# Output projection in three split passes through the piece ring, and a filter layer of two full-depth passes

## The reference

```python
merged = sigmoid(g_diff) * (o_diff @ w_proj_diff) + sigmoid(g_mla) * (o_mla @ w_proj_mla)
x = x + merged @ w_out                      # 512x1024 @ 1024x1024: the output projection
...
h = sin(freq * (h @ f_w3 + f_b3))           # 512x64
h = (h @ f_wout).reshape(L, 2, D_MODEL)     # the filter's last layer, 64 deep
h = h * exp(-t * |deltas|)                  # the decay
```

## Time and profile before

| | us |
|---|---|
| median of 3 runs (lowest, highest) | 1130.77 (1129.69, 1133.97) |
| the profiled execution | 1134.14 |
| its span | 1132.2 |
| merging of the attentions ends on PE | about 412.9 |
| first tile of the output projection | 414.70 to 421.64 |
| first turned tile of the next stage | 508.11 |

### The profile page before, as it was taken

How to read it: one execution, slowest core, us unless ns; L and a number is a source line. 1 busy time by engine, 2 the same in 40 slices (tenths; PEclk the granted TensorE clock), 3 DMA queues, 4 the chain that set the end, 5 groups by cost and what they waited for, 6 DMA issues and landing times.

```text
span 1132.2 us, 13210 instructions
## 1 busy us (share of the span) xinstructions
PE 1084.9 (96%) x4906; PEld 852.2 (75%) x4906; DVE 663.4 (59%) x1006; ACT 398.7 (35%) x624; POOL 513.9 (45%) x383
## 2 busy tenths in 40 slices
PE   6999989999899999998999989989999999999996
PEld 5889877766777864446788877867888888888885
DVE  6554759875487652388487784447666666640203
ACT  5223645453554201353443333143322223231211
POOL 1067989999200001150543335443555455464441
PEclk9999999999999999899999999989999999999999
DMA  6246354242344940330221211321222212322421
GB/s 243 75 159 227 109 211 160 84 159 85 130 149 164 372 157 0 130 130 1 93 75 75 76 75 72 151 94 67 84 75 106 116 74 83 139 75 75 149 75 75
DMA packets 17782, 131.41 MB, mean 116 GB/s; under 512 B 2289, under 2 KB 2689, under 8 KB 11138
## 3 DMA queue, kind: packets, MB, share of 16 engines
q1 hardware_dynamic: 8720, 93.21, 21.9%
q0 software_dynamic: 6560, 27.27, 7.2%
q10 hardware_dynamic: 2450, 10.21, 2.3%
HBM read 124.40 MB, written 6.29 MB: 115 GB/s over the span
## 4 chain that ended last, share of the span: by engine, by line
PE 87%; DVE 6%; ACT 3%; DMA 2%; issue 1%; POOL 1%; SPq 0%; ACTq 0%; POOLq 0%; DVEq 0%
PE bank L484 70%; PE bank L475 9%; PE bank L490 2%; PE bank L705 2%; DMA ring<-weights_in 1%; PE bank L703 1%; PE bank L702 1%; PE bank L851 1%; DMA x_sb<-x_in 1%; PE bank L820 1%; ACT arena L1070 1%; POOL ring_parts L1533 0%; ACT arena L1045 0%; PE bank L707 0%; ACT arena L1181 0%
## 5 line engine op out<-in xcount | busy, mean ns | idle before, releaser
L1533 POOL TENSOR_TENSOR ring_parts<-ring,ring_parts 128x1024 fp32r<-128x1024 f32 x98 | 237.8, 2430 | 299.2 <-ACT ring_parts L1045 298.9
L484 PE MATMUL bank<-hT_parts,ring_parts 128*128 128x512 f32 x1344 | 340.4, 394 | 0.5 <-ACT hT_parts L1317 0.5
L1045 ACT ACTIVATE ring_parts<-ring 128x1024 fp32r<-128x1024 f32 (+2 forms) x155 | 160.4, 1041 | 478.0 <-PE bank L484 298.5
L484 PEld LDWEIGHTS bank<-hT_parts,ring_parts 128*128 128x128 f32 x1344 | 250.5, 189 | 54.4 <-issue 2.4
L484 PE MATMUL bank<-ring_parts,arena_parts 128*128 128x512 f32 (+1 forms) x672 | 155.7, 386 | 1.5 <-DVE arena L2124 0.8
L484 PE MATMUL bank<-arena_parts,ring_parts 128*128 128x512 f32 x592 | 147.8, 391 | 2.9 <-DVE arena L1715 2.6
L484 PEld LDWEIGHTS bank<-ring_parts,arena_parts 128*128 128x128 f32 x672 | 124.5, 188 | 27.2 <-DVE arena L2124 1.3
L484 PE MATMUL bank<-ring_parts,hT_parts 128*128 128x512 f32 (+1 forms) x544 | 138.7, 379 | 0.3
L2227 DVE SCALAR_TENSOR_TENSOR arena<-bank,small,arena 128x441 f32<-128x441 f32 (+2 forms) x176 | 122.3, 695 | 23.8 <-DVE arena L2222 0.3
L484 PEld LDWEIGHTS bank<-arena_parts,ring_parts 128*128 128x128 f32 x592 | 111.0, 188 | 28.3 <-DVE arena L1715 2.8
L1630 DVE TENSOR_TENSOR ring_parts<-ring,ring_parts 128x1024 fp32r<-128x1024 f32 (+2 forms) x57 | 80.8, 1436 | 84.3 <-ACT ring_parts L1045 84.3
(11 more groups left out here) (227 smaller groups left out, 1141.2 us busy)
## 6 DMA issues: line engine op xcount, KB each, us to landing
ring<-weights_in SPq DMA_DIRECT2D x39, 2048.0 KB, 8.0
arena<-mod_w_in POOLq DMA_DIRECT2D x32, 512.0 KB, 4.1
arena<-mod_w_in POOLq DMA_DIRECT2D x8, 1024.0 KB, 4.9
ring<-weights_in SPq DMA_DIRECT2D x5, 512.0 KB, 9.1
x_sb<-x_in SPq DMA_DIRECT2D x4, 512.0 KB, 5.7
mod_spill<-mod_part POOLq DMA_DIRECT2D x16, 128.0 KB, 2.1
arena<-mod_spill ACTq DMA_DIRECT2D x1, 2048.0 KB, 15.4
x_sb<-x_in ACTq DMA_DIRECT2D x4, 512.0 KB, 18.8
```

Source lines behind the costliest of these rows:

```text
L484: ins = nc.tensor.matmul(out, l, r, start=start and n == 0, stop=stop and n == len(passes) - 1)
L1045: return nc.scalar.activation(out, in_, ACT.Copy)
L1533: return nc.gpsimd.tensor_tensor(part(low), low, part(high), ALU.subtract)
```

## The change

- `wo_tile` becomes 24 split matmuls (`product3`). The left operand is `sgd` in two parts: the high part is a ScalarE copy into `hT`, the low part is made in place by GpSimd. `C_WO0` and `C_WO1` become pieces of the ring: highs on ScalarE; lows of the first four pieces on VectorE among its merges, of the second four on GpSimd. The first tile of each half is ordered by passes (all high x high, all high x low, all low x high) with a wait at each block or piece.
- `filter_tile` becomes 2 x 2 split matmuls of 128 rows: `h3T` holds the high part of the sine network's output on partitions 0 to 63 and the low part on 64 to 127, against `wout_high` and `wout` (the low), both on all partitions. The network's last layer is therefore computed twice, side by side (`f_w3` is doubled). `C_FOUT` goes to the arena as 1 MB, right behind `C_WO0`, and its sums and splits are in two halves `n`.
- The order on PE is written out anew, with filter tiles later; the order on the other engines is changed to suit. `FIRST_HYZ` pieces now wait for the last pieces of `C_WO1`, and all their lows are behind the roots on GpSimd. Some loads are moved or joined.

```diff
             def wo_tile(i):
...
-                product(bank[i % 2], [(sgd[:, k, m * P:(m + 1) * P], cols(C_WO0 + n, k, 0, 512))
-                                      for k in range(KD)]).then_inc(sem("wo_done"), 1)
+                if m == 0:
+                    for k in range(KD):
+                        if n == 0:
+                            pe.wait_ge(sem("sgd_high"), k + 1)
+                        if k % 2 == 0:
+                            pe.wait_ge(sem("piece_high"), p + k // 2 + 1)
+                        product3(out, lefts[k:k + 1], rights[k:k + 1], start=k == 0, stop=False, terms=((0, 0),))
+                    for k in range(KD):
+                        if k % 2 == 0:
+                            pe.wait_ge(sem("piece_low"), p + k // 2 + 1)
+                        product3(out, lefts[k:k + 1], rights[k:k + 1], start=False, stop=False, terms=((0, 1),))
+                    for k in range(KD):
+                        if n == 0:
+                            pe.wait_ge(sem("sgd_low"), k + 1)
+                        ins = product3(out, lefts[k:k + 1], rights[k:k + 1], start=False, stop=k == KD - 1, terms=((1, 0),))
+                    ins.then_inc(sem("wo_done"), 1)
+                elif m < TT - 1:
+                    product3(out, lefts, rights).then_inc(sem("wo_done"), 1)
...
             def filter_tile(i):
...
-                    ins = nc.tensor.matmul(bank[b], h3T[:, t * P:(t + 1) * P], wout[d][n], start=True, stop=True)
+                    nc.tensor.matmul(bank[b], h3, part(wout_high[n][:, c]), start=True, stop=False)
+                    ins = nc.tensor.matmul(bank[b], h3, part(wout[n][:, c]), start=False, stop=True)
...
+            wo_tile(0)
+            modulation(0)
+            wo_tile(1)
+            modulation(1)
+            filter_tile(0)
+            wo_tile(2)
+            modulation(2)
+            filter_tile(1)
+            wo_tile(3)
+            modulation(3)
+            filter_tile(2)
+            filter_tile(3)
+            wo_tile(4)
+            wo_tile(5)
+            filter_tile(4)
+            wo_tile(6)
+            filter_tile(5)
+            abs_norm(0)
+            wo_tile(7)
+            filter_tile(6)
+            filter_tile(7)
...
# ScalarE
+            for d in range(KD):
+                wait("merge_out", KD + d + 1)
+                copy(part(hT[:, d, :]), sgd[:, d, :]).then_inc(sem("sgd_high"), 1)
+                if d % 2:
+                    split_high(FIRST_WO + d // 2)
+                if d == 4:
+                    wout_split(0)
...
+            modg_copy(2)
+            for p in range(FIRST_WO + PIECES, FIRST_HYZ):
+                split_high(p)
+            modg_copy(3)
...
+            wout_split(1)
             for m in range(TT):
                 square_x1(m)
...
# GpSimd
+            wait("fout_in", 16)
+            sum_wout(0)
+            for d in range(KD):
+                wait("sgd_high", d + 1)
+                subtract(sgd[:, d, :], hT[:, d, :]).then_inc(sem("sgd_low"), 1)
+            low_wout(0)
+            for p in range(FIRST_WO + PIECES, FIRST_HYZ):
+                split_low(p)
+            wait("modc_done", 4)
+            sum_wout(1)
+            low_wout(1)
             for m in range(TT):
                 wait("squares_done", squares_at("x1", m))
                 rsqrt(RS + m, SS + m, 1, D, "x_rs")
                 wait("squares_done", squares_at("x2", m))
                 rsqrt(RS2 + m, SS2 + m, 1, D, "x2_rs")
-                if m == 0:
-                    split_low(FIRST_HYZ)
-                if m < TT - 1:
-                    split_low(FIRST_HYZ + m + 1)
+            for p in range(FIRST_HYZ, FIRST_HYZ + PIECES):
+                split_low(p)
...
# VectorE
+            wait("net_out", 4)
+            V.tensor_tensor(part(h3T[FW:P, :]), net[0][FW:P, :], part(h3T[FW:P, :]), ALU.subtract).then_inc(sem("h3_ready"), 1)
...
                 V.tensor_tensor(sgd[:, d, :], sgd[:, d, :], sgm[:, d, :], ALU.add).then_inc(sem("merge_out"), 1)
                 if d == 3:
                     mod_chunk(7)
+                if d >= 5:
+                    split_low(FIRST_WO + d - 5)
+            split_low(FIRST_WO + 3)
```

More of the change, by code:

```diff
@@ L320, in build_program @@
         pieces += [(C_PD + j // 4, j % 4, "merge_done", 2 * (j + 1)) for j in range(8)]
+        FIRST_WO = len(pieces)
+        for n in range(2):
+            pieces += [(C_WO0 + n, j, "wo_piece", 3 * n + j + 1) for j in range(3)] + [(C_WO0 + n, 3, "wo_done", TT * (n + 1))]
         FIRST_HYZ = len(pieces)
@@ new lines, in wo_tile @@
+                lefts, rights = [], []
+                for k in range(KD):
+                    low, high = piece_parts(p + k // 2)
+                    c = slice(512 * (k % 2), 512 * (k % 2) + 512)
+                    lefts.append((hT[:, k, tokens], sgd[:, k, tokens]))
+                    rights.append((high[:, c], low[:, c]))
+                take(i % 2, "wo_out", i + 1)
+                if m == 0:
+                    for k in range(KD):
[8 more added lines that the diff above has]
+                        product3(out, lefts[k:k + 1], rights[k:k + 1], start=False, stop=False, terms=((0, 1),))
+                    for k in range(KD):
+                        if n == 0:
[4 more added lines that the diff above has]
+                    product3(out, lefts, rights).then_inc(sem("wo_done"), 1)
+                else:
+                    for q in range(PIECES):
+                        two = slice(2 * q, 2 * q + 2)
+                        ins = product3(out, lefts[two], rights[two], start=q == 0, stop=q == PIECES - 1)
+                        ins.then_inc(sem("wo_piece" if q < PIECES - 1 else "wo_done"), 1)
@@ L1052, in split_high @@
                     chunk_landed(act, pieces[p][0], 4 * past)
-                if p == FIRST_HYZ:
-                    wait(*chunk_used[C_FOUT])
-                elif p >= PIECES and not FIRST_HYZ < p < FIRST_HYZ + PIECES:
+                if p >= PIECES:
                     name, count = piece_done(p - PIECES)
@@ L1089, in net_out @@
                 wait("net_angle", i + 1)
-                nc.scalar.activation(net[0][0:FW, :] if i < 2 else h3T, net[1][0:FW, :], ACT.Sin).then_inc(sem("net_out"), 1)
+                rows = slice(0, FW if i < 2 else P)
+                nc.scalar.activation(net[0][rows, :], net[1][rows, :], ACT.Sin).then_inc(sem("net_out"), 1)
+                if i == 2:
+                    wait("net_out", 3)
+                    copy(part(h3T), net[0]).then_inc(sem("net_out"), 1)
             def input_out(i):
@@ L2188, in _ @@
             inverse_out(7)
[L2189 removed]
+            wait("row_in", 16)
             for i in range(2 * TT + 1):
@@ L2330 @@
         put(C_HYO + n, a["hy_w_out_2"][0][:, 512 * n:512 * n + 512])
-    stream[C_FOUT, 0:FW, 0:2 * D] = a["hy_f_wout_2"][0]
+    for half in (0, FW):
+        stream[C_FOUT, half:half + FW, 0:2 * D] = a["hy_f_wout_2"][0]
     hy = a["hy_w_in_2"][0]
@@ L2373 @@
     early[0:FW, EARLY["f_w2"]] = a["hy_f_w2_2"][0]
[L2374 to L2377 removed]
+    early[0:FW, EARLY["f_w3"]] = np.concatenate([a["hy_f_w3_2"][0]] * 2, axis=1)
+    for half in (0, FW):
+        for i in range(3):
+            small[half:half + FW, SMALL["f_b"].start + i] = a[f"hy_f_b{i + 1}_2"][0]
+        small[half:half + FW, SMALL["freq"].start] = a["hy_freq_2"][0]
     rowed = np.zeros((P, N_ROWED), f32)
```

155 lines of the change are left out of this document (78 added, 77 removed).

## The result

| | before | after |
|---|---|---|
| median (lowest, highest) of 11 runs each, us | 1133.8 (1129.69, 1136.66) | 1138.55 (1136.8, 1142.63) |
| ratio after to before, 95% interval | | 1.0053 [1.0035, 1.0071] |
| profiled execution, its span | 1134.14, 1132.2 | 1142.63, 1140.8 |
| mean granted clock in it | 0.992 | 0.981 |

The change makes the kernel slower by half a per cent. The forecast was no change (1131.5, range 1119 to 1139). The time lies in the range, but the forecast of no change was wrong. Of the 11 executions of the kernel after, the profiled one is the slowest, 4.1 above their median, so its trace overstates the loss: 8.6 us between the two spans, 4.75 between the medians.

A forecast was written before the change was run, and what follows sets the result against it. The prediction took the stage's end to hang on hand-overs between VectorE, ScalarE and GpSimd, despite PE being 96% busy. Four segments summed to 509.0 against 508.11, +0.9 on the median, put at 1131.5 us, range 1119 to 1139.

The forecast's parts named there:

- Segment A: Stage up to the first projected tile's end: 432.5 against 421.64 before, including +2.2 for half clock on PE.
- 8 us or more: Sign of being right: VectorE's last modulation chunk, mod_chunk 7, takes this long in place of 4.12 us.
- 8 or more: Sign of being right: PE stands 8 us or more between 413 and 426, released by ScalarE's copies or VectorE's subtractions.
- parts taken at nothing: Items priced at no cost: work after the stage, GpSimd's HYZ lows, moved loads and tables, doubled network layer, joined wait.
- the average row's +0.61: Contention price up to VectorE's last subtraction: +0.61 us on each of 17 operations beside GpSimd, 10.4 us in all.
- Segments B and C: B, to tile 3's end: 26.1 us, before 32.8. C, on to norm_x2(0): 19.5 us, before 20.1.
- Segment D: From norm_x2(0) to the first turned block: 30.9 us against 33.6 before, ending at 509.0.
- GpSimd's four HYZ lows end some 15 us before PE wants them: GpSimd's low parts for the next stage, 9.7 us of work, priced at no cost.
- After the stage every engine does what it did, 0.9 later.: Behind the first turned block: nothing changes except a shift of 0.9 us.
- slower by a clock that falls three times: Rival, chance 0.23: PE's waits in A, tile 4 and ahead of the spectrum bring half clock, +6 to +7; 1138.
- Contention is mild: Rival, chance 0.22: GpSimd's subtractions fit between VectorE's, A ends at 423, B at 449.5, the stage at 497.5; 1120.
- PE decides: Rival, chance 0.10: the handing round in D keeps up with PE, most of 20 us arrive; 1111 to 1116.

The follow-up runs named there:

- pool_after_mod: Changed kernel with GpSimd's sums and subtractions of the stage held until VectorE's last modulation chunk is done; 1136.47 us, ratio 1.0027 to before.
- hyz_late: Changed kernel with GpSimd's four low parts for the next stage held until the second norm's last row block is scaled; 1137.11 us, ratio 1.0027 to before.
- before_again: The kernel before, unchanged, run once more for a second trace; 1133.77 us.
- warm_late: Changed kernel with unread PE products in two waits behind the stage, near 526 and 562 us; 1133.92 us, ratio 1.0010 to before.
- filter_alone: Changed kernel with the projection put back to full-precision products, so only the filter's passes are split; 1140.49 us, ratio 1.0069 to before.
- wo_alone: Changed kernel with the filter's last layer put back to full-precision products, so only the projection is split; 1144.67 us, ratio 1.0120 to before.
- again: The changed kernel, unedited, run again for a second trace; 1139.07 us, ratio 1.0068 to before.
- mod_ahead: Changed kernel with the modulation's 32 columns and first broadcast on PE ahead of the first projected tile; 1135.16 us, ratio 0.9997 to before.
- best1: Changed kernel with modulation columns ahead of the first tile, GpSimd's stage work behind the last modulation chunk, next-stage lows behind the last scaling; 1129.26 us, ratio 0.9964.
- warm: Changed kernel with nine unread PE products in the first projected tile's two waits; 1134.32 us, ratio 1.0008 to before.

## Why the prediction was wrong

**Segment A: right in what it named, and its end met by luck.** Against the untouched wait the changed trace runs 3.1 later than before's, so I take 3.1 off. VectorE's last subtraction ends at 429.9 - 3.1 = 426.8 (forecast 427.5), the tile at 431.2 (432.5). The chunk took 8.13 ("8 us or more"), PE stood 10.1 ("8 or more"), and half clock ran on to 432. What I put among the "parts taken at nothing" was not nothing: the filter's weights and the decay distances are in flight beside the chunk's own weights, which take 2.9 us longer to land, and the chunk starts 2.25 late (2.10 in pool_after_mod). The forecast met the tile's end because its price of contention was too high by about as much: the average row's +0.61 gave 10.4 for the 17 operations, less 1 for idle time. They cost about 6.3: 4.0 for the eight steps (4.9 at +0.61), 1.8 for the five sums and 0.5 for the four piece subtractions. Two errors of 2 to 3 us cancelled.

The Trainium skill, "SBUF — State Buffer", section "Who interferes with whom", has the two engines' instructions exclude each other. The traces agree that they hold each other up: 8.13 us with GpSimd beside, 4.13 with GpSimd held back. They do not show full turns: GpSimd's records cover 6.3 of the 8.13 us, and with the 4.12 of the steps alone that would make 10.4 us.

**Segments B and C held.** B was 26.2 (460.53 - 434.31) for 26.1, C 19.2 for 19.5 (norm_x2(0) at 479.71). C's chain on GpSimd was as put, four pieces in 9.81, the sums 3.00 and the low part 2.40; PE's wait in tile 4 was 2.00 instead of 5.

**Segment D: a step failed.** It was 30.1 for 30.9, but only because the rest of the handing round was quicker than put; inside it lies a loss that I had at nothing. "GpSimd's four HYZ lows end some 15 us before PE wants them" looked at who waits for their results and not at whom they block: started behind the last root, they stand beside the last scaling, 2.82 instead of 0.75, which is on the path. hyz_late shows it, with a stage 0.7 to 1.0 shorter.

**The step that made the forecast wrong: "After the stage every engine does what it did, 0.9 later."** From the first turned block on it took 5.45 us more than in before's trace (156.71 for 151.26), then 1.5 more behind the next wait. Four falls of the clock, at 510, 526, 565 and 666, go with that; before_again prices two of them at 3.4. Between the second traces of both kernels, with three falls there after the change and two before it, only 1.5 is left (156.2 for 154.7), and 2.2 more is in the stage. That the clock is the cause and not a companion is shown by warm_late: with full clock behind two of these waits that stretch takes 152.8 and the median is 4.6 lower. The sum had priced half clock only once, +2.2 in segment A, and at nothing everywhere else. I had read one trace of before, in which the waits of 2.76 and 2.47 passed at full clock, as how these waits always pass, and had taken "before, 1.8 us of waiting cost nothing" for a bound. before_again shows the same waits with the fall.

**The rival that came nearest** is "slower by a clock that falls three times", to which I gave 0.23. Its forecast was 1138, its condition more than 8 us at 0.5 between 413 and 508; measured 1138.55, and 10 us in the window 422 to 432 alone. Its mechanism held, its places only in part: behind the first tile yes, in tile 4 no, then at 489 and at 510. It put its 6 to 7 us into the stage, which in the profiled pair got 1.5 shorter, so that 1138 for 1138.55 is luck in part. What I should have weighed, as I now read the traces, is that half a dozen waits of 2 to 3.7 us each draw for the clock, so that its cost grows with the number of waits rather than with the longest.

**"Contention is mild" and "PE decides"** fell with the 8.13 and with filter_alone and wo_alone. PE's plain products of the projection are gone from its timeline, as forecast, and its busy time fell by 9.4 instead of 20, half clock having stretched the rest.

**Slips in the working.** The average row's sum for VectorE's end is 418.6 + 9.4 = 428.0 and not 427; a MB at 2.5 us is not in the rows named with it (2 MB took 8.2 there, 4.1 each); and the mild rival's segment B ends at 423 + 26.1 = 449.1 and not 449.5. None of them moves the forecast by more than 0.5 us.

What stays open: why the falls near 526 and 562 came in seven each of the nine traces of changed kernels that leave those waits unfilled, and in about half the executions of the kernel before, if its groups by clock are read that way. The earlier parts of the traces differ too: the untouched wait came at 298.1 to 304.8 over all sixteen, with falls at 152 and from 294 to 302 in code that no experiment's edit touches, and the change itself only in one wait for constants. Nine of the 13 traces with the change or a part of it have at least one of these falls, none of the three of the kernel before; three traces are too few to say whether the change has a part in it. In this pair that stretch is 3.1 us of the 8.6.

## What to carry to other kernels

Work taken from an engine that is busy 96% of the time can come back as waits on it, if a hand-over between three others is nearly as long; here those waits were then followed by half clock on the engine that had been relieved. Before such a change, list the new waits and ask of each what could stand in it: needed wide matmuls first, unread ones if there are none. And ask of every operation that is moved off the path whom it blocks, not only who wants its result; and read two profiles of the kernel before, since one shows a single draw.

## What was not expected of the hardware

- The clock falls behind waits as short as 1.9 to 2.8 us, but not each time: the same wait of 2.76 us was passed at 1.00 in one execution of the kernel before and at half clock in the next. Longer ones passed too: 3.15 us at 486.83 in again and 3.38 at 498.80 in mod_ahead, both at 1.00.
- The clock fell where PE never stood. In best1, 64 records of matmuls with one moving column, back to back, lay in a stretch at 0.60, and took 0.169 us each instead of 0.115. Sixteen such records between products passed at full clock elsewhere (1.84 us at 434.31 in the kernel after).
- The waits of warm were not filled whole. With products in 4.4 of 5.7 us and in 3.6 of 4.4 the clock stayed at 1.00 across the gaps of 1.6 and 1.5 us that were left.
